# Giving back four weight slots in three parts instead of four, and choosing experts in fewer vector steps

## The reference

```
g_logits = xt @ w_rg + b_rg                   # 4 groups
g_idx    = argmax(g_logits)                   # one group for each token
e_logits = (xt @ w_re + b_re).reshape(T, 4, 8)
e_sel    = e_logits[token, g_idx]             # the 8 experts of that group
top_p, top_i = top_k(softmax(e_sel), 2)       # two experts for each token
weights  = p_g * top_p / sum(top_p)
# each chosen expert e: (silu(x @ w_gate_e[e]) * (x @ w_up_e[e])) @ w_down_e[e]
# out = sum of the two experts' rows, weighted; then the residual and the second block
```

## Time and profile before

| | |
|---|---|
| median of 3 runs | 778.24 us (778.0 to 778.46) |
| profiled execution, its own time | 778.07 us |
| its span, first to last instruction | 776.3 us |
| PE, DVE, ACT busy, share of the span | 94%, 54%, 44% |
| HBM read in the span | 204.18 MB |
| mean granted TensorE clock | 0.988 |

### The profile page before, as it was taken

How to read it: one execution, slowest core, us unless ns; L and a number is a source line. 1 busy time by engine, 2 the same in 40 slices (tenths; PEclk the granted TensorE clock), 3 DMA queues, 4 the chain that set the end, 5 groups by cost and what they waited for, 6 DMA issues and landing times.

```text
span 776.3 us, 12463 instructions
## 1 busy us (share of the span) xinstructions
PE 731.0 (94%) x5138; PEld 601.7 (78%) x5138; DVE 420.0 (54%) x747; ACT 337.9 (44%) x604; POOL 32.4 (4%) x65
## 2 busy tenths in 40 slices
PE   8999999999999999999675879999999999999997
PEld 8898888888788866666343549999778888888885
DVE  5667756667666421111010208666668776777675
ACT  5966565554444421110010127555656434344433
POOL 2700000000000000000000001000001000000000
PEclk9999999999999999999988999999999999999999
DMA  8953557347988899999999998953434464555201
GB/s 340 415 211 118 206 218 285 120 165 285 372 311 333 342 350 420 421 419 420 421 420 421 413 417 352 422 203 115 157 109 163 159 221 163 193 186 188 84 1 54
DMA packets 34170, 206.07 MB, mean 265 GB/s; under 512 B 4032, under 2 KB 4416, under 8 KB 12352
## 3 DMA queue, kind: packets, MB, share of 16 engines
q1 hardware_dynamic: 34112, 205.25, 68.3%
HBM read 204.18 MB, written 1.05 MB: 264 GB/s over the span
## 4 chain that ended last, share of the span: by engine, by line
PE 79%; DMA 12%; ACT 3%; SPq 3%; DVE 2%; issue 1%; DVEq 0%; POOLq 0%; POOL 0%; ACTq 0%
PE ps L679 43%; PE ps L749 10%; PE ps L752 5%; PE ps L1067 4%; DMA ext<-in_w_up_e 4%; DMA big<-in_w_gate_e 3%; DMA X<-in_w_down_e 3%; PE ps L1090 2%; PE ps L1003 2%; SPq L496 2%; DMA gb<-in_xT 2%; PE ps L1100 1%; PE ps L1192 1%; PE ps L1206 1%; PE ps L1220 1%
## 5 line engine op out<-in xcount | busy, mean ns | idle before, releaser
L1769 DVE TENSOR_TENSOR wl<-raw,wh 128x1024 fp32r<-128x1024 f32 (+3 forms) x181 | 213.3, 1195 | 135.1 <-ACT wh L1352 133.8
L1352 ACT CAST wh<-raw 128x1024 fp32r<-128x1024 f32 (+3 forms) x181 | 181.9, 1024 | 66.4 <-PE ps L679 42.6
L679 PE MATMUL ps<-wh,fra 128*128 128x512 f32 (+3 forms) x636 | 179.2, 367 | 0.5 <-DVE gb L1978 0.5
L679 PEld LDWEIGHTS ps<-wh,fra 128*128 128x128 f32 x636 | 112.8, 189 | 18.2 <-issue 1.0
L679 PE MATMUL ps<-wl,fra 128*128 128x512 f32 (+3 forms) x318 | 115.1, 362 | 0.0
L749 PE MATMUL ps<-fra,wh 128*128 128x512 f32 x352 | 110.7, 396 | 0.7 <-DVE fra L1780 0.7
L752 PEld LDWEIGHTS ps<-fra,wl 128*128 128x128 f32 x352 | 66.1, 188 | 15.5
L679 PE MATMUL ps<-fra,wh 128*128 128x256 f32 x400 | 74.0, 286 | 0.5 <-DVE wl L1769 0.5
L679 PE MATMUL ps<-wh,frb 128*128 128x512 f32 x240 | 74.3, 391 | 0.0
L752 PE MATMUL ps<-fra,wl 128*128 128x256 f32 x352 | 69.2, 278 | 0.0
L679 PEld LDWEIGHTS ps<-wl,fra 128*128 128x128 f32 x318 | 59.9, 188 | 9.0
(11 more groups left out here) (282 smaller groups left out, 992.3 us busy)
## 6 DMA issues: line engine op xcount, KB each, us to landing
raw<-in_dense SPq DMA_DIRECT2D x79, 1024.0 KB, 5.1
ext<-in_w_down_e SPq DMA_DIRECT2D x20, 1024.0 KB, 19.0
raw<-in_w_gate_e SPq DMA_DIRECT2D x17, 1024.0 KB, 25.0
ext<-in_w_up_e SPq DMA_DIRECT2D x14, 1024.0 KB, 24.5
big<-in_w_up_e SPq DMA_DIRECT2D x8, 1024.0 KB, 18.7
big<-in_w_gate_e SPq DMA_DIRECT2D x7, 1024.0 KB, 26.9
raw<-in_w_up_e SPq DMA_DIRECT2D x6, 1024.0 KB, 20.4
raw<-in_dense SPq DMA_DIRECT2D x9, 512.0 KB, 5.3
```

Of the source, the lines that this page charges most:

```text
L679: t = e.matmul(o, a, w, start=first and n == 0, stop=final and n == 2, skip_group_check=not check)
L1352: e.copy(halves(q)[0], piece_view(q)).then_inc(*up("wh", q))
L1769: e.tensor_tensor(l, piece_view(q), h.bitcast(F), ALU.subtract).then_inc(*up("wl", q))
```

## The change

Three edits go together. The four slots are given back in three parts: two quarters after gate steps 0 and 1, as before, and then the remaining half after gate step 3, in place of a quarter after step 2 and one after step 3; the weights of these slots lie in HBM to match. The router does with one SCALAR_TENSOR_TENSOR (subtract, then add) what two instructions did, by way of a rank table scaled by 1e30; it negates the maximum after the MATCH_REPLACE; TensorE takes the rank of both halves of the tokens in one product of 64 columns, to which the product with ones is added; and `select` is one instruction for both halves, for all eight groups. Of the four unread products before the first gather two stay.

```
-WARM = (9, 6, 9, 10, 4, 6)
+PARTS = (0, 512), (512, 1024), (1024, 2048)
+WARM = (9, 6, 9, 10, 2, 6)
-    c[:, C_RANK:C_RANK + 4] = 4 - np.arange(4)
+    c[:, C_RANK:C_RANK + 4] = -NEG * (4 - np.arange(4))
...
-            for a in range(4):
+            for n, (a, b) in enumerate(PARTS):
                 for u in wt.parted:
-                    e.wait_ge(*(at("taken", "part", a) if a < 3 else released(wt.before[u])))
+                    e.wait_ge(*(at("taken", "part", n) if n < 2 else released(wt.before[u])))
...
-        e.matmul(bank[2][:, 0:32], tri, M[:, 0, :], start=True, stop=True)
-        e.matmul(bank[2][:, 32:64], ones, M[:, 0, :], start=True, stop=False)
-        e.matmul(bank[2][:, 32:64], tri, M[:, 1, :], start=False, stop=True).then_inc(*up("rank"))
+        e.matmul(bank[2][:, 0:64], tri, M.rearrange("p i n -> p (i n)"), start=True, stop=False, skip_group_check=True)
+        e.matmul(bank[2][:, 32:64], ones, M[:, 0, :], start=False, stop=True, skip_group_check=True).then_inc(*up("rank"))
...
-            t.then_inc(*(up("taken", "part", n) if n < 3 else up("taken", "eg", 0)))
+            if n != 2:
+                t.then_inc(*(up("taken", "part", n) if n < 2 else up("taken", "eg", 0)))
...
-            t = e.tensor_scalar(OG[:, i, :], OG[:, i, :], tm_[:, i, :], NEG, ALU.is_lt, ALU.mult)
-        t.then_inc(*routed())
-        e.wait_ge(*own())
-        for i in range(2):
-            t = e.tensor_tensor(EM[:, i, :].rearrange("p (g k) -> p g k", g=4),
-                                el[:, i, :].rearrange("p (g k) -> p g k", g=4),
-                                OG[:, i, :].unsqueeze(2).to_broadcast([P, 4, 8]), ALU.add)
+            t = e.scalar_tensor_tensor(EM[:, i, :].rearrange("p (g k) -> p g k", g=4),
+                                       OG[:, i, :].unsqueeze(2).to_broadcast([P, 4, 8]), tm_[:, i, :],
+                                       el[:, i, :].rearrange("p (g k) -> p g k", g=4), ALU.subtract, ALU.add)
...
-        e.tensor_scalar(nm, top[:, :, 0:1], -1.0, None, ALU.mult).then_inc(*up("expert maximum"))
         e.memset(top[:, :, 2:8], ABSENT).then_inc(*routed())
...
-        e.wait_ge(*own())
+        taken = own()
+        e.tensor_scalar(nm, top[:, :, 0:1], -1.0, None, ALU.mult).then_inc(*up("expert maximum"))
+        e.wait_ge(*taken)
         e.tensor_scalar(M, TT, TAKEN, None, ALU.is_equal).then_inc(*up("M"))
...
-            for i in range(2):
-                t = e.tensor_tensor(hots[i], iota, of_four(PX[:, i, :], g), ALU.is_equal)
-            t.then_inc(*up("sel", g))
+            e.tensor_tensor(hot.rearrange("p (i e s) -> p i e s", i=2, e=4), iota.unsqueeze(1).to_broadcast([P, 2, 4, CAP]),
+                            PX[:, :, 4 * g:4 * g + 4].unsqueeze(3).to_broadcast([P, 2, 4, CAP]), ALU.is_equal).then_inc(
+                *up("sel", g))
```

More of the change, by code:

```diff
@@ L174, in plan @@
         for u, z in enumerate(self.slot):
-            times[z] = times.get(z, 0) + (64 if u in self.parted else 16)
+            times[z] = times.get(z, 0) + (48 if u in self.parted else 16)
             self.nth.append(times[z])
@@ L191, in laid @@
                 self.begin[u] = n
-                parts.append(np.ascontiguousarray(src.reshape(P, 4, 512).transpose(1, 0, 2)).reshape(-1))
-                n += parts[-1].size
+                for a, b in PARTS:
+                    parts.append(np.ascontiguousarray(src.reshape(P, 2048)[:, a:b]).reshape(-1))
+                    n += parts[-1].size
         return np.concatenate(parts)
@@ L498, in fetch_parted @@
         def fetch_parted():
-            for a in range(4):
+            for n, (a, b) in enumerate(PARTS):
                 for u in wt.parted:
-                    e.wait_ge(*(at("taken", "part", a) if a < 3 else released(wt.before[u])))
-                    first = wt.begin[u] + 512 * P * a
-                    e.dma_start(slot_view(u).rearrange("p k n -> p (k n)")[:, 512 * a:512 * a + 512],
-                                dense[first:first + 512 * P].rearrange("(p m) -> p m", p=P)).then_inc(s_slot[wt.slot[u]], 16)
+                    e.wait_ge(*(at("taken", "part", n) if n < 2 else released(wt.before[u])))
+                    e.dma_start(slot_view(u).rearrange("p k n -> p (k n)")[:, a:b],
+                                dense[wt.begin[u] + P * a:wt.begin[u] + P * b].rearrange("(p m) -> p m", p=P)).then_inc(
+                        s_slot[wt.slot[u]], 16)
         def fetch_last_up():
```

## The result

| | before | after |
|---|---|---|
| median of 22 runs, us | 778.43 (777.03 to 779.87) | 781.05 (776.97 to 783.49) |
| profiled execution, us | 778.07 | 782.38 |
| its span, us | 776.3 | 780.6 |
| its mean granted clock | 0.988 | 0.983 |

The ratio after to before is 1.0031, 95% interval 1.0020 to 1.0041. The kernel became slower by 2.6 us, where 1.3 us of gain were forecast. The runs also scatter more: 6.5 us from lowest to highest, against 2.8.

What follows compares the result with a forecast made beforehand. The prediction took the DMA weight stream, short of 420 GB/s at 274 to 290 us, as the bound. Gains of 0.97 + 0.3 + 0.07 = 1.34 us gave a 776.9 us median, 8-in-10 range 775.9 to 777.9.

Steps and rivals of the forecast that it cites:

- Two go (0.57 us): Before the first gather: two unread products removed, freeing TensorE ahead of `hot`, so up to 0.29 us more is saved.
- one goes: Router's rank: one of five 32-column products, 0.22 us each, is removed; saving 0.20 us (0.15 to 0.22).
- the whole stake of 3.12 us: Weight stream, 274 to 290 us: 1312 KB lost against 420 GB/s, the most a change there could win.
- the expert stage ends when the last down matrix lands: Expert stage: the products wait for this matrix, landing at 461.94 us; every us given back to the stream ends it earlier.
- The mask and the negation: Router: fewer mask instructions save 0.26 us (0.16 to 0.39); the moved negation saves 0.11 (-0.06 to 0.11).
- Rival D: Queue runs empty before the late half; 0.7 us wait plus some 1 us restart: 779.9 us, chance 0.04.
- Rival E: Fewer unread products let TensorE's clock fall to 1.2 GHz at gathers and gate steps: 782 us, chance 0.02.
- 0.82 us of the 1.60 lost in the first 4 us comes back directly: Start of the stream: earlier gates return this, plus some slow restart; taken 0.97 us, bounds 0.3 and 1.6.
- 0.37 for the middle and the rows: Stream: fewer requests recover 0.3 us of the middle's 1.14 loss; larger rows of the halves give 0.07.
- C: Rival: earlier start buys little because the second request's 1.07 us stall persists; gain 0.3 to 0.5, 777.8 us, chance 0.14.
- A: The forecast itself: gain 1.34 us, 776.9 us, own range 776.4 to 777.4, chance 0.60.
- The parts: Two quarters and a half: four fewer SP issues worth nothing; gain from fewer requests 0.3 us, larger rows 0.07.

Runs made afterwards that it cites:

- e1: Changed kernel with three unread products (12 TensorE instructions) put at the start of group 3's gates, ahead of the jump; 777.35 us, ratio 0.9991 to before.
- e2: Kernel before with 64 unread products (256 TensorE instructions) added inside the general path, which is skipped; 782.87 us, ratio 1.0076 to before.
- e4: Kernel before with the change's quarters and halves alone, router and unread products as before; 777.96 us, ratio 1.0003 to before.
- e6: Kernel before with five unread products at the start of the gates of each of groups 1 to 6; 779.39 us, ratio 1.0009 to before.
- e16: Further execution of the kernel before, unchanged, profiled for its clock at the router; 776.90 us.
- e17: Further execution of the kernel before, unchanged, profiled for its clock at the router; 778.12 us.
- e5: Changed kernel with the four quarters of before and three unread products at group 3's gates; 777.57 us, ratio 0.9988 to before.
- e8: Changed kernel with four unread products behind the counts again, not two, and one more at group 3's gates; 777.71 us, ratio 0.9993 to before.
- e9: Changed kernel with three of the ten unread products ahead of the ranks left out; 778.21 us, ratio 1.0006 to before.
- e14: Further execution of e9's kernel, profiled; 781.54 us.
- e7: Changed kernel without the general path on TensorE, and so without its jump; 777.53 us, ratio 0.9989 to before.
- e10: Changed kernel with six unread products (24 instructions) at group 3's gates; 777.34 us, ratio 0.9989 to before.
- e12: Changed kernel with two unread products (8 instructions) at group 3's gates; 777.48 us, ratio 0.9988 to before.
- e18: Further execution of the kernel before, unchanged, profiled for its clock at the router; 778.16 us.

## Why the prediction was wrong

**The step that failed** is the cost of the TensorE instructions taken out: "Two go (0.57 us)", "one goes". They were priced by the time that they took. That the program behind them moves by 12 instructions had no term, and no rival spoke of the jump over the general path. That one missing term is 3.1 us by the ratios of the changed kernel and of e1, as much as the whole stake of 3.12 us. The path failed with it: by the prediction "the expert stage ends when the last down matrix lands", and from 353 us on the chain lies in DMAs. In fact 75.9 of the 108 us up to that landing are DMAs, the rest is SP and TensorE, and TensorE was only 2.67 us of waits ahead of the stream when the jump cost it 5.66 more.

The Trainium skill has the rule that bears on this, in "Runtime: NRT & Kernel Launch", section "Instruction fetch mechanics": the program comes in blocks of 16 KiB, the next one is fetched ahead only in sequence, and a taken branch whose target isn't in the window forces a fetch before execution goes on. The traces agree: 5.9 us where the target was late. A branch over a path that isn't run is a taken branch here; that reading was missed.

**What held.** The mask and the negation: the rank products start 0.28 + 0.09 = 0.37 us earlier against the router's start, forecast 0.26 + 0.11. The pair at 0.41 (0.42). `hot` ready at 271.52, 0.57 + 0.09 = 0.66 earlier (0.64). The gather 0.80, or 0.89 against the router's start (0.82). SP at 274.69 (274.7): against the router's start that is 0.90 earlier (0.82), and that the router began 0.09 late brought the time itself so near, which is luck. The halves at 279.73 (279.7) with 0.66 us of idle SP (0.7). Rival D stayed away: the stream had 409 GB/s at 282 to 290 and did not run dry. Rival E is not what made the profiled execution slow: its clock at the router was 1.00, and fell only behind the new wait.

**What was mis-sized.** "0.82 us of the 1.60 lost in the first 4 us comes back directly", taken as 0.97 with the restart, and 0.37 for the middle and the rows. In the changed kernel 0.34 us came back by the stretches: the shortage moved on into the middle, 272 GB/s for 300, and the start was slow again, 2.00 us for three issues where the next lot takes 1.39. Over 274 to 290 us the traces without a fall of the clock have, with the router of before, 338 GB/s (before), 348 (e2), 339 (e4), 333 (e6), 338 and 337 (e16 and e17), and with the changed router 347 (changed kernel), 357 (e5), 354 (e8), 362 and 371 (e9 and e14): in the mean 19 GB/s more, which over 16 us is 0.7 us of stream, with single traces of the two kinds as near as 348 and 347. And where the clock falls at the router, most of the earlier start itself goes, since the slack that covered it is gone; the working did not price that. By the runs, e1, e5, e7, e8 and e10 to e12 lie 0.0007 to 0.0012 under before, 0.5 to 0.9 us, each with an interval of some 0.8 us to either side: between C's 0.3 to 0.5 and A's 1.34.

**The parts**: forecast 0.37 of gain; e4's ratio says 0.2 us of loss, with an interval from 0.5 of gain to 0.9 of loss. Undecided, and not needed: e5 without them is as fast as e1.

Kernels with the jump put right are clearly faster than the changed kernel, and about 0.1% faster than before: e10, 777.34 us, 0.9989 [0.9979, 0.9999], and e5 without the parts, 0.9988 [0.9978, 0.9998].

## What to carry to other kernels

Where a program jumps over a path, count the instructions that an edit adds or removes ahead of the jump, on that engine, and look behind the jump for idle time put down to "issue" together with the queue of instructions: its transfer should begin some 3 us ahead of the work that needs it. If a change that is right by every row comes out slower and scatters more, put an unread product or two ahead of the jump (4 or 8 instructions here), or take the jump away, before the change itself is judged. And price a start of a stream by the stretch that it fills: a request issued 0.8 us earlier gave back 0.34 us in the changed kernel's trace and some 0.7 in the mean of the traces, not the forecast 1.34, since the shortage moved behind it.

## What was not expected of the hardware

- Instructions that never run cost time: 256 of them inside a skipped path made the kernel 0.76% slower [0.48%, 1.04%] (e2, six runs).
- A missed target costs TensorE 5.7 to 5.9 us, 2.9 to 3.0 until the transfer begins and 2.9 from there, though the transfer itself takes 1.1 (the 2.3% of 16 engines' 3 us above).
- The wait then costs more than itself: the granted clock behind it is 0.51 for five us.
- The wait is not fixed for a program: 0.24, 2.28 and 5.87 us in three executions of one kernel.
- The granted clock falls at the router in some executions of one kernel and not in others (1.00, 1.00, 0.88 over 262 to 276 us in e16 to e18).
